# A hybrid encoder layer with 16,384 retrieved experts: other beats for the second sequence's stages

## The chip, the cores and the metric

One core of a Trainium2 chip runs the whole program. The metric is the time of one execution on the device, in microseconds (us). It is given as the median of the runs, and beside it stands the one execution that was profiled.

## What is computed

Two sequences of 512 tokens (width 1024) pass the same layer, in float32. The reference, cut to what matters here:

```python
def encoder_layer(x, ...):
    xn = rmsnorm(x, norm1_g)
    a, hy, gates = split(xn @ w_in)                       # 512, 1536, 2048 columns
    ya = multiscale_pool(a) @ w_pool_out
    yb = hyena_mixer(hy) @ w_hyena_out                    # short conv, FFT conv, products
    h = x + (sigmoid(gate_a) * ya + sigmoid(gate_b) * yb) @ w_o
    return h + peer(rmsnorm(h, norm2_g))

def peer_block(xb):                                       # 128 tokens
    s = einsum(q(xb), keys)                               # 8 heads, 2 x 128 scores each
    sv, si = top_k(s, 16); best, pos = top_k(all 256 pair sums, 16)
    idx, gate = ids of the 128 chosen experts, softmax(best)
    act = gelu(einsum('ted,td->te', u_tab[idx], xb)) * gate
    return einsum('te,ted->td', act, v_tab[idx])
```

## The kernel before

`first_sequence` runs the first sequence alone up to its keys' scores (0 to 629.7 us in the trace). `second_and_experts` then does two things at once: the layer of the second sequence, and the experts of all 1024 tokens, in 8 tiles of 128 tokens. It holds all that the change touches.

**Gathered tiles** (0, 1, 5, 6, 7). For each of 128 choices POOL fetches one row of `peer_u` per token (`fetch_u`, L1359, 512 KB) and DVE multiplies it with the tokens and sums (`dot`, L1686). The row of `peer_v` (`fetch_v`, L1369, 512 KB) is weighted and summed by PE: `quad` (L1472) takes four choices in 8 matmuls. There are 6 buffers for rows of u and 7 for rows of v.

**Dense tiles** (2, 3, 4). All 16,384 experts are computed, in 128 steps: `product` (L1435, 8 matmuls, a 512 KB block of the first table), a gelu on ACT, the weighting on DVE, and for four steps 6 `job`s (L1451, 4 matmuls each, blocks of `peer_v`), which DVE adds up (L1724). The weights of the 16,384 experts for these tiles are built before that, in 48 chunks of 8 tokens: DVE and ACT write one-hot rows (L1671, L1538, L1546), PE multiplies them (`gates`, L1423), ACT evicts.

**Beats.** Every engine's queue is written out by hand in a loop over beats `n`. Beat `n` fetches row `n` of u (640 in all) and row `n - LAG` of v (LAG = 134). So beats 0 to 133 fetch only u, beats 134 to 639 fetch both, and beats 640 to 773 only v. The queues are in order; a beat has no duration of its own.

**Ticks.** The stages of the second sequence stand in each queue by ticks of 1.5 us of nominal cost (`Walk.upto`): z (8 weight blocks), f (the transform), i (its inverse), a/x/mix (pools), ga/gb/o (24 weight blocks), r (16 half blocks), t2 (transposes), and at last q and s, after which DVE routes two heads for tiles 4 and 5 (`route_here`). `tick_of` says how many ticks stand before a beat, `beat_of` is its inverse:

```python
def tick_of(n, lag, rows):
    return min(n, lag) + 2 * max(0, min(n, rows) - lag) + max(0, n - rows)
```

The other work is placed in beats: `ROUTED` (tile, first beat, pace: one `route_head` each, L139 to L161), `RANKED_AT` (`chosen`: the pass that turns ranks into expert numbers, L167 to L190), `GATED_AT` (the softmax's sum), `CHUNK_AT` (the 48 chunks). `FIRST` is the tick of the first dense step, `PACE` the ticks between two, and the last falls 16 ticks ahead of `TICKS`.

## Time and profile before

| what | value |
|---|---|
| median of 3 runs | 3322.87 us |
| range of the runs | 3322.39 to 3337.04 us |
| profiled execution | 3342.03 us, its span 3340.2 us |
| mean granted TensorE clock | 0.939 |
| busy: PE, DVE, POOL, ACT | 2901.8, 1731.4, 1532.3, 554.3 us |
| DMA traffic | 1004.79 MB, mean 301 GB/s |

Busy times overlap: each engine has the whole span. The clock is the share of full speed that was granted. GB/s counts all queues together; the DMA share beside it is the mean busy share of the 16 DMA engines, and it can pass 1 when packets overlap.

### The profile page before, as it was taken

How to read it: one execution, taken by the hardware profiler on the slowest of the kernel's cores; microseconds unless marked ns; L12 is line 12 of the kernel's file. 1: busy time of each engine (PE TensorE's matmuls, PEld its weight loads, DVE VectorE, ACT ScalarE, POOL GpSimd, SP SyncE). 2: the span in 40 equal slices, each digit the busy share in tenths (PEclk: the TensorE clock that was granted, in tenths of full speed). 3: DMA queues.
4: the chain of work that ended last, by engine and by line, in shares of the span. 5: the costliest groups of instructions: out<-in, count | busy, mean ns of one | idle time of the engine just before them, and what ended most of it. 6: DMA issues, size and time to landing. Idle time of an engine off the chain costs nothing.

```text
span 3340.2 us, 29711 instructions
## 1 busy us (share of the span) xinstructions
PE 2901.8 (87%) x10143; PEld 1457.6 (44%) x10143; DVE 1731.4 (52%) x3842; ACT 554.3 (17%) x1188; POOL 1532.3 (46%) x1335
## 2 busy tenths in 40 slices
PE   5999989566779989855599999999999999999995
PEld 3656648222334445424244444444444444443331
DVE  4331028789984746688347744466644444441101
ACT  3211123000124535436100000000000000000000
POOL 2211112365555544436455555555556555553343
PEclk9999989778889989977799999999999999999998
DMA  3332353797888998868999999999989999997786
GB/s 129 117 104 72 123 179 107 247 354 237 269 327 305 350 387 327 320 252 320 389 360 390 369 382 377 385 400 385 380 326 384 395 371 376 386 366 288 278 295 229
DMA packets 343933, 1004.79 MB, mean 301 GB/s; under 512 B 31751, under 2 KB 114567, under 8 KB 341224
## 3 DMA queue, kind: packets, MB, share of 16 engines
q0 software_dynamic: 184320, 671.17, 53.4%
q1 hardware_dynamic: 157736, 306.57, 25.8%
q10 hardware_dynamic: 1728, 25.17, 1.9%
q8 instruction: 81, 1.33, 0.2%
q14 instruction: 68, 0.56, 0.0%
HBM read 950.62 MB, written 52.17 MB: 300 GB/s over the span
## 4 chain that ended last, share of the span: by engine, by line
PE 55%; DMA 8%; DVE 8%; issue 4%; ACT 3%; POOL 2%; another core or an unknown queue 1%; SPq 1%; DVEq 0%; ACTq 0%; POOLq 0%
PE job_ps L1451 19%; PE wide_ps L1435 18%; PE v_ps L1472 8%; PE wide_ps L579 3%; DMA v_rows<-in_peer_v,row_t 3%; DMA tmp_gates<-arena 2%; PE job_ps L579 2%; PE gate_ps L1423 2%; DVE prod L1686 2%; DMA u_row<-in_peer_u,row_u 2%; ACT arena L1546 1%; POOL u_row L1359 1%; ACT arena L1538 1%; DMA arena<-in_w_o 1%; DVE prod L186 1%
## 5 line engine op out<-in xcount | busy, mean ns | idle before, releaser
L1369 POOL DMA_INDIRECT v_rows<-in_peer_v,row_t x640 | 673.2, 1052 | 799.6 <-PE v_ps L1472 624.8
L1359 POOL DMA_INDIRECT u_row<-in_peer_u,row_u x640 | 736.5, 1151 | 487.3 <-DVE dots L1686 278.2
L1686 DVE CUSTOM_DVE_ANT_0 prod<-u_row,x_tile 128x1024 f32<-128x1024 f32 x640 | 766.2, 1221 | 88.3 <-DMA u_row<-in_peer_u,row_u 76.4
L1435 PE MATMUL wide_ps<-arena 128*128 128x384 f32 x2048 | 691.6, 492 | 32.0 <-DMA arena<-in_peer_ut 32.0
L1451 PE MATMUL job_ps<-arena 128*128 128x512 f32 x1536 | 692.7, 599 | 1.5 <-DVE arena L1724 0.9
L1435 PEld LDWEIGHTS wide_ps<-arena 128*128 128x128 f32 x2048 | 386.9, 191 | 353.7 <-issue 84.0
L1451 PEld LDWEIGHTS job_ps<-arena 128*128 128x128 f32 x1536 | 288.5, 191 | 377.3 <-issue 349.6
L1472 PE MATMUL v_ps<-v_rows,diag 128*32 128x512 f32 x2560 | 365.5, 619 | 54.5 <-DMA v_rows<-in_peer_v,row_t 37.4
L1724 DVE TENSOR_TENSOR arena<-arena,job_ps 128x512 f32<-128x512 f32 x192 | 131.9, 687 | 512.2 <-PE job_ps L1451 413.6
L843 POOL TENSOR_TENSOR exact<-arena,exact 128x1024 fp32r<-128x1024 f32 x48 | 117.8, 2457 | 445.2 <-ACT exact L591 445.2
L1572 ACT ACTIVATE arena<-wide_ps 128x384 f32<-128x384 f32 x128 | 62.7, 490 | 1492.8 <-PE wide_ps L1435 1218.9
L1712 DVE TENSOR_TENSOR arena<-arena 128x384 f32<-128x384 f32 x128 | 71.4, 558 | 374.8 <-ACT arena L1572 337.7
L579 PE MATMUL wide_ps<-arena 128*128 128x512 f32 x528 | 243.7, 618 | 18.0 <-DVE arena L785 18.0
L1472 PEld LDWEIGHTS v_ps<-v_rows,diag 128*32 128x32 f32 x2560 | 75.6, 111 | 286.2 <-issue 194.5
L579 PEld LDWEIGHTS wide_ps<-arena 128*128 128x128 f32 x528 | 103.6, 200 | 147.9 <-issue 147.7
L579 PE MATMUL job_ps<-arena 128*128 128x512 f32 x368 | 165.7, 605 | 0.0
L99 PE MATMUL pre_ps<-exact 128*128 128x512 f32 x384 | 159.5, 415 | 2.0 <-DVE exact L738 2.0
L1423 PE MATMUL gate_ps<-arena 128*128 128x128 f32 x640 | 99.0, 304 | 64.0 <-ACT arena L1561 42.8
L100 PE MATMUL pre_ps<-exact 128*128 128x512 f32 x384 | 151.1, 393 | 0.0
L101 PE MATMUL pre_ps<-exact 128*128 128x512 f32 x384 | 150.9, 393 | 0.0
L1423 PEld LDWEIGHTS gate_ps<-arena 128*128 128x128 f32 x640 | 90.2, 212 | 101.3 <-issue 93.2
L1546 ACT ACTIVATE arena<-arena,gate_t,gate_n 128x128 f32<-128x128 f32 x320 | 127.4, 482 | 0.9
(242 smaller groups left out, 2263.9 us busy)
## 6 DMA issues: line engine op xcount, KB each, us to landing
arena<-in_peer_ut SPq DMA_DIRECT2D x128, 512.0 KB
arena<-in_peer_v SPq DMA_DIRECT2D x128, 512.0 KB
arena<-in_w_in SPq DMA_DIRECT2D x64, 512.0 KB, 3.6
tmp_gates<-arena ACTq DMA_DIRECT2D x12, 2048.0 KB
arena<-tmp_gates SPq DMA_DIRECT2D x32, 768.0 KB
arena<-in_w_o SPq DMA_DIRECT2D x32, 512.0 KB, 3.6
arena<-in_wq SPq DMA_DIRECT2D x32, 512.0 KB, 4.7
u_row<-in_peer_u,row_u POOLq DMA_INDIRECT x640
```

Of the source, the lines that this page charges most:

```text
L99: pe.matmul(out, w_lo, m_hi, start=first, stop=False)
L100: pe.matmul(out, w_hi, m_lo, start=False, stop=False)
L101: return pe.matmul(out, w_hi, m_hi, start=False, stop=last)
L579: return pe.matmul(out, self.w_raw[r][:, c], moving[0][:, k], start=first, stop=last)
L1359: pool.indirect_dma_start(u_row[n % NU][:], None, dram["peer_u"], bass.IndirectOffsetOnAxis(row_u[g % 2][:, e:e + 1], 0)).then_inc(u_in[n ...
L1369: pool.indirect_dma_start(v_row[n % NV], None, dram["peer_v"], bass.IndirectOffsetOnAxis(row_t[g % 3][:, t:t + 1], 0)).then_inc(v_in[n % N ...
L1423: last = pe.matmul(gate_bank(c, u)[:].rearrange("p (a t) -> p t a", t=4)[:, v], hot_b[c % 2][:, 4 * u + v], hot_a[c % 2][:, 4 * u + v], st ...
L1435: last = pe.matmul(wide[j % 2][:, 0:TD], uw[j % NW][:, k * P:(k + 1) * P], x_t[:, k], start=k == 0, stop=k == KD - 1)
L1451: last = pe.matmul(job_ps[q % 2][:], actd[g % 2][:, jj, d * P:(d + 1) * P], vw[j % NO][:, half * 512:(half + 1) * 512], start=jj == 0, sto ...
L1472: last = pe.matmul(v_ps[half][32 * q:32 * q + 32, :], diag[:, q, 32 * c:32 * c + 32], v_row[r % NV][:, half * 512:(half + 1) * 512], start ...
L1546: last = act.activation(hot_b[c % 2][:, v], hot_b[c % 2][:, v], ACT.Relu, bias=gate_t[d % 2][:, t0 + v:t0 + v + 1], scale=gate_n[d % 2][:, ...
L1686: dve.tensor_tensor_reduce(out=prod[n % 2][:], in0=u_row[n % NU][:], in1=xb[g % 2][:], scale=1.0, scalar=0.0, op0=ALU.mult, op1=ALU.add, a ...
```

## The change

It changes what a beat stands for, and moves the work that is placed in beats. In beats 0 to 133 two ticks stand where one stood; in beats 134 to 639 two as before; after them one as before.

```diff
 def beat_of(tick, lag, rows):
-    if tick < lag:
-        return int(tick)
-    if tick < lag + 2 * (rows - lag):
-        return int(lag + (tick - lag) / 2)
-    return int(rows + tick - lag - 2 * (rows - lag))
+    return int(tick / 2) if tick < 2 * rows else int(rows + tick - 2 * rows)
 def tick_of(n, lag, rows):
-    return min(n, lag) + 2 * max(0, min(n, rows) - lag) + max(0, n - rows)
+    return 2 * min(n, rows) + max(0, n - rows)
...
-    TICKS = 2 * ROWS
+    TICKS = 2 * ROWS + LAG
...
-    ROUTED = ((2, 72, 8), (3, 134, 7), (6, LAST + 60, 5), (7, 420, 8))
-    RANKED_AT = (-1, 64, 133, 187, LAST + 1, LAST + 4, LAST + 104, 484)
-    GATED_AT = (1, 72, 140, 194, LAST + 3, LAST + 10, LAST + 110, 492)
+    ROUTED = ((2, 36, 6), (3, 92, 6), (6, LAST + 90, 8), (7, 420, 8))
+    RANKED_AT = (-1, 30, 82, 140, LAST + 1, LAST + 4, LAST + 156, 484)
+    GATED_AT = (1, 36, 90, 148, LAST + 3, LAST + 10, LAST + 162, 492)
...
-    CHUNK_AT = [144 + 3 * c for c in range(EARLY // 2)]
-    CHUNK_AT += [198 + 3 * c for c in range(EARLY // 2)]
+    CHUNK_AT = [94 + 3 * c for c in range(EARLY // 2)]
+    CHUNK_AT += [152 + 3 * c for c in range(EARLY // 2)]
     CHUNK_AT += [max(CHUNK_AT[-1] + 3, GATED_AT[4]) + 3 + c + c // 2 for c in range(EARLY // 2)]
...
-    FIRST = LAG + 2 * (CHUNK_AT[-1] + 6 - LAG)
+    FIRST = tick_of(CHUNK_AT[-1] + 6, LAG, ROWS)
```

Worked out, these beats move (the two functions carry `LAST`, the beat of the last unit, and `TURNED`, the one ahead of q):

| beat of | before | after |
|---|---|---|
| first q (`TURNED`) | 203 | 136 |
| last unit of the layer (`LAST`) | 248 | 181 |
| chunks 0 to 15, 16 to 31, 32 to 47 | 144 to 189, 198 to 243, 254 to 276 | 94 to 139, 152 to 197, 203 to 225 |
| first dense step | 282 | 231 |
| `FIRST`, `PACE` in ticks | 430, 6.32 | 462, 7.09 |
| last product | 726 | 722 |

No instruction is added or taken away. Line numbers of the changed kernel are 4 lower from here on (L1686 is L1682 there, L1472 is L1468, L1435 is L1431, L1451 is L1447, L1423 is L1419).

First place: DVE, between two stages of the transform (`prods` and `kf` lie in `diag`). Before:

```order
L781 TENSOR_TENSOR v_rows<-diag 128x512
L1686 ISA prod,dots<-u_row,x_tile 128x1024
L1686 ISA dots 128x1
L1686 ISA prod,dots<-u_row,x_tile 128x1024
L1686 ISA dots 128x1
L1686 ISA prod,dots<-u_row,x_tile 128x1024
L1686 ISA dots 128x1
L1686 ISA prod,dots<-u_row,x_tile 128x1024
L1686 ISA dots 128x1
L1686 ISA prod,dots<-u_row,x_tile 128x1024
L1686 ISA dots 128x1
L775 TENSOR_TENSOR diag<-wide_ps,diag 128x512
```

and now:

```order
L781 TENSOR_TENSOR v_rows<-diag 128x512
L1682 ISA prod,dots<-u_row,x_tile 128x1024
L1682 ISA dots 128x1
L1682 ISA prod,dots<-u_row,x_tile 128x1024
L1682 ISA dots 128x1
L1682 ISA prod,dots<-u_row,x_tile 128x1024
L1682 ISA dots 128x1
L775 TENSOR_TENSOR diag<-wide_ps,diag 128x512
```

Five dots stood between them, now there are two.

Second place: PE, in the stages ga, gb and o, whose weight blocks are L579. Before:

```order
L1423 MATMUL gate_ps<-arena 128x128 x4
L1472 MATMUL v_ps<-v_rows,diag 32x512 x8
L1423 MATMUL gate_ps<-arena 128x128 x4
L579 MATMUL wide_ps<-arena 128x512 x8
L1423 MATMUL gate_ps<-arena 128x128 x4
L579 MATMUL wide_ps<-arena 128x512 x8
L1423 MATMUL gate_ps<-arena 128x128 x4
L1472 MATMUL v_ps<-v_rows,diag 32x512 x8
L1423 MATMUL gate_ps<-arena 128x128 x4
L579 MATMUL job_ps<-arena 128x512 x8
```

and now:

```order
L1419 MATMUL gate_ps<-arena 128x128 x8
L579 MATMUL job_ps<-arena 128x512 x8
L1419 MATMUL gate_ps<-arena 128x128 x8
L579 MATMUL wide_ps<-arena 128x512 x8
L1419 MATMUL gate_ps<-arena 128x128 x4
L579 MATMUL wide_ps<-arena 128x512 x8
L1419 MATMUL gate_ps<-arena 128x128 x8
L579 MATMUL job_ps<-arena 128x512 x8
```

The quads (v_ps) are gone from these stages; the chunks' matmuls (gate_ps) are still in them.

Third place: PE in the dense stretch, some way in. Before:

```order
L1451 MATMUL job_ps<-arena 128x512 x4
L1435 MATMUL wide_ps<-arena 128x384 x8
L1451 MATMUL job_ps<-arena 128x512 x8
L1472 MATMUL v_ps<-v_rows,diag 32x512 x8
L1435 MATMUL wide_ps<-arena 128x384 x8
L1451 MATMUL job_ps<-arena 128x512 x8
L1472 MATMUL v_ps<-v_rows,diag 32x512 x8
L1451 MATMUL job_ps<-arena 128x512 x4
L1435 MATMUL wide_ps<-arena 128x384 x8
L1472 MATMUL v_ps<-v_rows,diag 32x512 x8
L1435 MATMUL wide_ps<-arena 128x384 x8
L1451 MATMUL job_ps<-arena 128x512 x8
```

and now:

```order
L1431 MATMUL wide_ps<-arena 128x384 x8
L1468 MATMUL v_ps<-v_rows,diag 32x512 x8
L1431 MATMUL wide_ps<-arena 128x384 x8
L1468 MATMUL v_ps<-v_rows,diag 32x512 x8
L1447 MATMUL job_ps<-arena 128x512 x8
L1431 MATMUL wide_ps<-arena 128x384 x8
L1468 MATMUL v_ps<-v_rows,diag 32x512 x8
L1447 MATMUL job_ps<-arena 128x512 x8
L1431 MATMUL wide_ps<-arena 128x384 x8
L1447 MATMUL job_ps<-arena 128x512 x4
L1468 MATMUL v_ps<-v_rows,diag 32x512 x8
L1431 MATMUL wide_ps<-arena 128x384 x8
```

A quad stands after fewer products and jobs. Counted over the whole order, 37 quads stand ahead of the first product before and 24 now; from there to the quad of beat 639 PE has 114 products, 165 jobs and 89 quads before, and 116, 168 and 102 now; after it 14 products, 27 jobs and 34 quads, and now 12, 24 and 34.

## Rows read from the trace of the kernel before

**Rows 1.** Busy time of the engines by stage, whole second half
```profile
core 0: us, PE busy (x) PEld busy (x) DVE busy (x) ACT busy (x) POOL busy (x), PEclk, DMA share, GB/s
629.70:793.90 164.20, 116.83 (x270) 52.62 (x268) 144.25 (x253) 8.81 (x13) 102.67 (x78) 0.85 0.88 317
793.90:906.00 112.10, 82.85 (x169) 35.31 (x170) 103.86 (x270) 10.12 (x14) 57.26 (x45) 0.84 0.81 269
906.00:1145.80 239.80, 209.28 (x750) 98.00 (x749) 164.26 (x397) 98.04 (x255) 133.44 (x114) 0.95 0.87 318
1145.80:1255.50 109.70, 89.37 (x325) 45.03 (x324) 62.76 (x98) 46.06 (x113) 51.43 (x47) 0.89 0.99 386
1255.50:1463.00 207.50, 184.69 (x810) 101.11 (x808) 139.16 (x450) 111.10 (x287) 97.52 (x86) 0.95 0.87 318
1463.00:1640.80 177.80, 68.65 (x389) 45.27 (x389) 123.54 (x252) 67.67 (x171) 86.07 (x74) 0.69 0.83 314
1640.80:3023.20 1382.40, 1357.06 (x4569) 632.93 (x4570) 706.31 (x1455) 67.30 (x127) 759.55 (x707) 0.99 0.99 376
3023.20:3340.20 317.00, 268.25 (x989) 101.23 (x987) 43.80 (x74) 12.41 (x24) 121.72 (x129) 0.95 0.75 270
```

**Rows 2.** Timeline of PE: start, us, engine, line, what; idle before it in brackets
```profile
701.53 1.97 PE L508 MATMUL wide_ps<-s_ident,arena 128*128 128x128 f32 x8 [18.24 <-DVE arena L754]
...
745.77 3.75 PE L527 MATMUL wide_ps<-arena,v_rows 128*128 128x512 f32 x4 [10.42 <-DVE diag L778]
...
793.88 6.65 PE L579 MATMUL wide_ps<-arena 128*128 128x512 f32 x10 [18.02 <-DVE arena L785]
```

**Rows 3.** Timeline of PE in the dense stretch: products, jobs, quads
```profile
1690.23 1.92 PE L1472 MATMUL v_ps<-v_rows,diag 128*32 128x512 f32 x16
1692.09 5.43 PE L1435 MATMUL wide_ps<-arena 128*128 128x384 f32 x16
1697.35 7.03 PE L1451 MATMUL job_ps<-arena 128*128 128x512 f32 x16
1704.22 5.32 PE L1435 MATMUL wide_ps<-arena 128*128 128x384 f32 x16
1709.38 3.60 PE L1451 MATMUL job_ps<-arena 128*128 128x512 f32 x8
```

**Rows 4.** Timeline of PE where the layer's last weights and the gates alternate
```profile
1103.92 7.03 PE L579 MATMUL job_ps<-arena 128*128 128x512 f32 x16
1110.79 1.05 PE L1423 MATMUL gate_ps<-arena 128*128 128x128 f32 x8
1111.78 0.64 PE L1472 MATMUL v_ps<-v_rows,diag 128*32 128x512 f32 x4
```

**Rows 5.** Timeline of DVE after the layer's last unit
```profile
1460.42 1.23 DVE L1686 CUSTOM_DVE_ANT_0 prod<-u_row,x_tile 128x1024 f32<-128x1024 f32 x1 [0.25 <-DVE rk_best_at L161]
...
1461.58 1.22 DVE L1686 CUSTOM_DVE_ANT_0 prod<-u_row,x_tile 128x1024 f32<-128x1024 f32 x1
...
1469.46 0.49 DVE L139 MAX8 rk_top<-arena 128x8 f32<-128x128 f32 x2
...
1475.23 0.29 DVE L167 CAST top_key<-rk_top_at 128x256 f32<-128x256 uint32 x1 [0.21 <-DVE rk_best_at L161]
...
1490.92 1.23 DVE L1686 CUSTOM_DVE_ANT_0 prod<-u_row,x_tile 128x1024 f32<-128x1024 f32 x1 [0.25 <-DVE key L190]
```

**Rows 6.** Timeline of POOL, one gather of a row per token
```profile
1609.24 0.94 POOL L1369 DMA_INDIRECT v_rows<-in_peer_v,row_t  x1 [0.30 <-issue]
```

**Rows 7.** Busy time in three full pieces of the dense stretch
```profile
2100.00:2150.00 50.00, 50.00 (x169) 23.82 (x169) 19.50 (x33) 2.45 (x5) 27.80 (x27) 1.00 1.03 403
2200.00:2400.00 200.00, 199.14 (x683) 92.20 (x681) 116.83 (x297) 7.84 (x16) 107.57 (x104) 1.00 1.01 388
2580.00:2600.00 20.00, 20.00 (x63) 9.07 (x62) 8.89 (x15) 0.98 (x2) 9.53 (x10) 1.00 1.03 410
```

**Rows 8.** Waits of PE after the last dot
```profile
PE v_ps L1472 <- DMA v_rows<-in_peer_v,row_t: 23.6, 24, 4.0
```

**Rows 9.** DMA queue of the gathers: packets, MB, share of 16 engines
```profile
q0 software_dynamic: 184320, 671.17, 53.4%
```

More of the change, by code:

```diff
@@ L1145, in second_and_experts @@
     EARLY = CHUNKS // ND * 2
-    ROUTED = ((2, 72, 8), (3, 134, 7), (6, LAST + 60, 5), (7, 420, 8))
-    RANKED_AT = (-1, 64, 133, 187, LAST + 1, LAST + 4, LAST + 104, 484)
-    GATED_AT = (1, 72, 140, 194, LAST + 3, LAST + 10, LAST + 110, 492)
-    assert 194 < LAST and LAST + 106 < 3 * P
-    CHUNK_AT = [144 + 3 * c for c in range(EARLY // 2)]
-    CHUNK_AT += [198 + 3 * c for c in range(EARLY // 2)]
+    ROUTED = ((2, 36, 6), (3, 92, 6), (6, LAST + 90, 8), (7, 420, 8))
+    RANKED_AT = (-1, 30, 82, 140, LAST + 1, LAST + 4, LAST + 156, 484)
+    GATED_AT = (1, 36, 90, 148, LAST + 3, LAST + 10, LAST + 162, 492)
+    assert 148 < LAST and LAST + 158 < 3 * P
+    CHUNK_AT = [94 + 3 * c for c in range(EARLY // 2)]
+    CHUNK_AT += [152 + 3 * c for c in range(EARLY // 2)]
     CHUNK_AT += [max(CHUNK_AT[-1] + 3, GATED_AT[4]) + 3 + c + c // 2 for c in range(EARLY // 2)]
```

## The prediction

> **What bounds the kernel now.** I read the busy time by stage first. It falls into two kinds. From 1640.8 to 3023.2 us, the dense stretch, PE is busy 1357 of 1382 us at a clock of 0.99 [rows 1]: PE is the bound. But the same row has a DMA share of 0.99 and 376 GB/s, so a second bound lies just behind. Ahead of it, from 629.7 to 1640.8 us, nothing is full for long: PE is busy 752 of 1011 us, DVE 738 (the first six rows of the group, summed), and they wait for each other. Until 906 us DVE is the fuller one (248 of 276 us, PE 200), because a dot stands in its queue for every 1.5 us of nominal stage work. The timeline of PE shows what that costs: 18.2, 10.4 and 18.0 us of idle time at the ends of z, f and i, each ended by a late DVE operation [rows 2]. From 906 to 1255.5 us PE is the fuller one (299 of 350 us), and from 1463 to 1640.8 us both wait: PE is busy 69 of 178 us.
>
> **Prices.** A product takes 5.16 us, a job 3.44 (two in 6.87), a quad 1.86, all from start to start [rows 3]. A weight block of the layer takes 6.87 us and half a chunk of gates 0.99, so a chunk about 1.95 [rows 4]. On DVE a dot takes 1.15 us, a routed head 5.8, a chosen pass 15.7 [rows 5]. A gather holds POOL for 0.94 + 0.30 us [rows 6] and moves 671.17 MB / 1280 = 0.524 MB [rows 9]. A dense step loads 1.245 MB: twice 512 KB, and a quarter of the 768 KB of gates for four steps.
>
> **The stretch up to the first q** takes 626 us now, with 203 dots, 17 quads and three chosen passes beside it. After the change 67 dots fewer (77 us of DVE), no quad (17 x 1.86 = 32 us of PE), and two chosen passes (16 us less). I go by stage.
> - z, f, i: 164.2 us now. PE's own work is 8 blocks (55 us) and 32 matmuls each for f and i, at a quarter of a job (27.5 us each), with the transposes 114. DVE has 39 dots in place of 78 (45 us less of 144). The chosen pass falls at beat 30, as i starts on PE: with nine dots, a head and the gate sum it is 33 us beside PE's 28 to 30, so the 18.0 us wait becomes about 5. I keep 20 us of the 50 in waits: **134**.
> - a, x, mix: DVE has 104 us in 112, of which 43 dots (50 us) and five heads (28). Now 21 dots (24), three heads (17) and the same 26: 67 us against PE's 59. They alternate closely, at the 0.87 that I take between them: **78**.
> - ga, gb, o: 239.8 us now. PE then has 165 us of blocks and 8 chunks (16), 181 in all, DVE about 150. The row has PE at 0.87 today; with the quads' row waits gone I take 0.91: **198**.
> - r and t2: 109.7 us now at 386 GB/s. PE's own work is 55 for r and 4 for t2, with seven chunks 73. Without the v rows the loads of w_o meet less traffic, and tile 3's chosen pass (16 us of DVE) has moved on: **94**.
>
> Sum 504, so 122 us less than 626. The bounds are 428 (PE alone: 399 us of stages and 15 chunks) and 549 (only the 77 us of dots gained).
>
> **q and s** still share two ticks per beat, 45 beats with both gathers, as before. One chosen pass and its gate sum come in (beat 140, 16 us), one chunk goes: 207.5 + 12 = **220**.
>
> **From the layer's end to the first product** there were 34 beats and now there are 50, since the second 16 chunks still stand beyond the layer's end in part and tile 4's 16 come after them. The 16 extra beats carry six chunks. POOL needs 2 x 1.24 = 2.5 us for each, the DMA 1.05 MB, 2.6 us at 400 GB/s, ACT some 2.7; I take 2.9. 178 + 46 = **224**. Here 46 us of the 122 are given back.
>
> So the first product starts at 629.7 + 504 + 220 + 224 = 1578, where it was 1641: **63 us earlier**.
>
> **The dense stretch** then has 51 beats more. PE: 116 x 5.16 + 168 x 3.44 + 102 x 1.86 = 1366 us, against 114, 165, 89: 1321, of the 1382 measured (0.956). At that share PE would need 1429, 47 us more. The DMA: today 376 x 1382 = 520 MB. Now 102 more gathers (53.5 MB) and two steps (2.5): 576 MB. What can the queues carry? The fullest 20 us show 410 GB/s, the fullest 50 us 403, the fullest 200 us 388, each at a share of 1.01 to 1.03 with PE at 100% [rows 7]. At 410 the 576 MB take 1405 us, which is above PE's 1366. **So the DMA takes over as the bound of this stretch.** At 403 it is 1429, at 388 1485. Between the dips at the tiles' borders and a queue that must not run dry, I take 395: 1458, rounded **1460**, 78 us more than now. Who waits then: dot waits for u rows, quad for v rows, and behind the waiting quad stand the products and jobs of PE.
>
> The Trainium skill (HBM Reference, Specifications) gives about 358 GB/s as a core's share, and about 425 for a core that streams alone. At 358 the stretch would take 1609 us and the change would be a clear loss; this trace has 376 over the whole stretch, so the lower figure does not bind here. At 425 it would be 1355 us, below PE's 1366, and PE would stay the bound; no 20 us of this trace show more than 410.
>
> **After the last dot** 12 products, 24 jobs and 34 quads are left where 14, 27 and 34 were: 2 x 5.16 + 3 x 3.44 = 21 us less of PE, in a stretch of 317 us where PE is busy 268 and waits 23.6 us in 24 pieces for v rows [rows 8]. A little of it turns into such waits: **20 us less**.
>
> **The sum**: -63 + 78 - 20 = -5 against the profiled execution, 3340.2 of span and 3342.0 in all. That one lies 19 us above the median (3322.9), 5 us above the highest of the runs; I take the same -5 from the median: **3318 us**.
>
> **Rivals.**
> 1. *The queues carry more than 403 GB/s* when they are asked for it, and PE stays the bound: 1429 instead of 1460, 31 us less, so 3287. For it: the shares never pass 1.03, and in the rows of 410 GB/s it was PE that was full, so nobody has asked for more. Against: three different pieces stop at 403 to 410. The same side is reached when the first stretch comes nearer to its PE bound: 480 instead of 504 gives 3294. Faster, together 0.36.
> 2. *The DMA gives 385*, as in the stages r and t2, where PE was busy only 89 of 110 us at a share of 0.99 [rows 1]: 576 / 385 = 1496, 36 us more than I take, so 3354. The mechanism is a queue of 6 and 7 buffers that stalls PE in order: a quad waits for four rows, and the products behind it wait too, so the loads of the next steps are issued later. It decides for slower from 390 GB/s down, given the other terms. Slower, 0.19.
> 3. *The DVE bursts stop PE in the first stretch*: two ticks per beat leave a unit of 6.87 us only 2.4 beats, and a head or a chosen pass in them is more than that slack. If PE's share there stays what it is today (498 of 626 us, 0.80), its 428 us take 535, 31 more than I have: 3349. Slower, 0.06.
> 4. My forecast, that the gain ahead of the first product is paid back behind it, 3301 to 3339: 0.39.
>
> **The chances.** A measurement of this kernel tells some 0.5% (16.6 us) from no change. Faster 0.36, same 0.39, slower 0.25. The range takes in 480 to 530 for the first stretch and 385 to 405 GB/s, not all at once: 3268 to 3360.
>
> **What the new profile would show.** Right: the first q at 1134 us, the last s at 1354, the first product near 1578, with DVE and PE both about 0.8 busy until the first q and no idle piece of 18 us before i's end is read. In the dense stretch PE below 0.95 busy, DMA 390 to 400 GB/s at 1.02, and DVE and PE waits for u and v rows many times the present ones; the last dot at 3038. Wrong: a dense stretch with PE at 0.98 (rival 1), or with less than 388 GB/s over it (rival 2), or a first q later than 1165 (rival 3). If the first product is not 40 to 85 us earlier, the first half of this working is what failed.

## The result, and the profile after

| | before | after |
|---|---|---|
| median (runs, range), us | 3322.63 (4, 3318.55 to 3337.04) | 3372.53 (4, 3362.45 to 3376.74) |
| ratio of the medians | | 1.0138, 95% interval 1.01 to 1.0176 |
| profiled execution, us | 3342.03 | 3362.45 |

The change makes the kernel 50 us slower. The forecast was 3318 and the range ended at 3360. The two profiled executions are 20 us apart and not 50: the one of before was 19 us above its median, the one of after 10 us below. So each kernel was profiled a second time; the stages of all four executions are below.

The stages of the changed kernel, cut at the same events as in [rows 1] (columns as there):

```profile
629.00:764.00 135.00, 112.68 (x269) 50.27 (x269) 98.54 (x176) 8.59 (x13) 51.71 (x42) 0.96 0.70 240
764.00:866.00 102.00, 97.13 (x212) 41.84 (x212) 85.38 (x222) 11.32 (x16) 38.71 (x30) 0.94 0.71 232
866.00:1015.40 149.40, 145.51 (x417) 70.67 (x416) 123.01 (x292) 56.05 (x143) 65.99 (x49) 1.00 0.76 262
1015.40:1118.40 103.00, 76.98 (x276) 43.33 (x274) 67.93 (x172) 61.31 (x156) 35.83 (x28) 0.90 0.85 318
1118.40:1319.50 201.10, 178.09 (x751) 93.03 (x752) 152.69 (x466) 96.57 (x244) 102.21 (x88) 0.94 0.87 325
1319.50:1554.40 234.90, 104.76 (x579) 62.17 (x577) 145.68 (x283) 104.92 (x276) 124.01 (x104) 0.70 0.85 320
1554.40:3058.80 1504.40, 1436.45 (x4853) 651.40 (x4853) 776.84 (x1570) 71.47 (x133) 893.86 (x810) 0.99 1.00 382
3058.80:3360.70 301.90, 249.55 (x914) 89.43 (x913) 40.15 (x70) 11.44 (x22) 121.26 (x129) 0.95 0.79 283
```

The seventh row is the one that counts. The dense stretch has grown from 1382 us to 1504, at 382 GB/s and a share of 1.00; PE is busy 0.955 of it, where it was 0.982. Ahead of it the change gains: the first product comes 86 us earlier. Laid beside the working (all in us; the pools and ga/gb/o stand together, because the border between them is not drawn at quite the same instruction in the two traces):

| stage | before | forecast | after | second execution: before, after |
|---|---|---|---|---|
| z, f, i | 164 | 134 | 135 | |
| a, x, mix, ga, gb, o | 352 | 276 | 251 | |
| r, t2 | 110 | 94 | 103 | |
| all ahead of the first q | 626 | 504 | 489 | 613, 493 |
| q, s | 208 | 220 | 201 | 208, 204 |
| to the first product | 178 | 224 | 235 | 177, 233 |
| dense stretch | 1382 | 1460 | 1504 | 1382, 1502 |
| after the last dot | 317 | 297 | 302 | 318, 304 |

In the second pair the sum is -67 ahead of the first product, +120 in the dense stretch and -14 after it: +39, and the times are 3327.58 and 3367.52.

In PE's timeline the three waits of [rows 2] read now (columns as there):

```profile
685.25 1.09 PE L508 MATMUL wide_ps<-s_ident,arena 128*128 128x128 f32 x8 [3.17 <-DVE arena L754]
...
723.44 1.95 PE L527 MATMUL wide_ps<-arena,v_rows 128*128 128x512 f32 x4 [3.10 <-DVE diag L778]
...
763.54 7.01 PE L579 MATMUL wide_ps<-arena 128*128 128x512 f32 x9 [12.29 <-DVE arena L785]
```

46.7 us have become 18.6. The first half of the change shortens these waits as intended.

The dense stretch is where the waits have grown. The waits there, first of the kernel before, then of the changed one (engine, tile, line, what it waited for: us in total, times, longest; PEld is PE's weight load):

```profile
PEld v_ps L1472 <- DMA v_rows<-in_peer_v,row_t: 16.6, 9, 4.8
DVE prod L1686 <- DMA u_row<-in_peer_u,row_u: 15.4, 9, 3.0
...
PE turn_ps L1391 <- DVEq L1646: 12.8, 2, 8.8
PE v_ps L1472 <- DMA v_rows<-in_peer_v,row_t: 10.7, 4, 3.9
```

```profile
POOL v_rows L1365 <- PE v_ps L1468: 342.8, 77, 31.7
...
DVE prod L1682 <- DMA u_row<-in_peer_u,row_u: 104.9, 65, 4.8
...
PEld v_ps L1468 <- DMA v_rows<-in_peer_v,row_t: 75.6, 38, 5.0
...
PE v_ps L1468 <- DMA v_rows<-in_peer_v,row_t: 44.3, 28, 4.1
PE turn_ps L1387 <- DVEq L1642: 16.1, 1, 16.1
```

A row of u is late 65 times where it was late 9 times, and a quad finds its rows missing 28 times in place of 4. POOL stands 343 us in front of gathers of v, because a quad on PE has not yet freed a buffer; in the kernel before that was 315 us. The row of PE's weight load says something that the row of PE hides. A quad needs four rows of v one after the other, and when the third or fourth is late, the wait can lie inside the quad and count as busy. In the grouping by line, the quads' matmuls take (busy, mean ns, idle before), in before and in after:

```profile
L1472 PE MATMUL v_ps<-v_rows,diag 128*32 128x512 f32 x1424 | 183.7, 605 | 10.9 <-DMA v_rows<-in_peer_v,row_t 10.7 <-issue 0.2
```

```profile
L1468 PE MATMUL v_ps<-v_rows,diag 128*32 128x512 f32 x1648 | 240.5, 608 | 44.3 <-DMA v_rows<-in_peer_v,row_t 44.3
```

1648 matmuls are 103 quads, and at 1.86 us each [rows 3] they need 192 us, not 240.5. That is 49 us more (before: 89 x 1.86 = 166 of 183.7, 18 us more). Some of it is waiting: the weight load waits 31 us longer for rows than the row of PE shows (75.6 and 44.3), and before only 6 us longer (16.6 and 10.7). The other 12 to 18 us are in both kernels.

Where in the stretch was traffic missing? Cut into five pieces:

```profile
1554.40:1854.40 300.00, 287.52 (x973) 130.78 (x974) 166.29 (x381) 14.86 (x28) 177.63 (x162) 0.98 1.02 392
1854.40:2054.40 200.00, 183.96 (x613) 82.34 (x612) 105.57 (x206) 10.24 (x18) 119.55 (x107) 0.98 0.95 362
2054.40:2454.40 400.00, 389.89 (x1324) 176.76 (x1323) 224.64 (x512) 18.31 (x35) 242.28 (x221) 1.00 1.02 394
2454.40:2604.40 150.00, 131.66 (x444) 60.82 (x443) 76.62 (x125) 8.10 (x14) 82.67 (x73) 0.94 0.88 334
2604.40:3058.80 454.40, 443.42 (x1506) 200.69 (x1504) 203.71 (x347) 19.96 (x38) 271.73 (x247) 1.00 1.01 389
```

Outside two holes the queues bring 392 GB/s (452 MB in 1154 us), close to the 395 of the working. In the holes, around the chosen passes of tiles 6 and 7, they bring 362 and 334: against 392 that is 200 x 30 + 150 x 58 = 14.7 MB, and 14.7 MB at 392 GB/s are 37 us. The two holes are as large as most of the 44 us by which this term was missed. The second lies around tile 7's pass, which the change does not touch (beat 484 in both kernels). The timelines of PE and of POOL there:

```profile
2477.99 1.92 PE L1468 MATMUL v_ps<-v_rows,diag 128*32 128x512 f32 x16
2496.03 0.47 PE L1387 MATMUL turn_ps<-s_ident,row_f 128*128 128x128 f32 x1 [16.12 <-DVEq L1642]
```

```profile
2481.44 1.62 POOL L1365 DMA_INDIRECT v_rows<-in_peer_v,row_t  x1 [0.30 <-issue]
2498.13 1.68 POOL L1355 DMA_INDIRECT u_row<-in_peer_u,row_u  x1 [15.07 <-DVE dots L1682]
```

While DVE turns ranks into expert numbers (15.7 us), it does no dot, no buffer of u comes free, and POOL stands 15 us in front of its next gather, with the gathers of v queued behind it. PE meanwhile waits 16 us for the row numbers that this pass makes. PE's idle piece as a window:

```profile
2480.00:2498.00 18.00, 1.97 (x4) 1.28 (x5) 17.45 (x23) 1.59 (x2) 2.56 (x2) 0.58 0.56 223
```

223 GB/s over 18 us. Whether such a hole is made up afterwards, the last experiments try. The pass isn't all that is in the holes: over the 200 and 150 us POOL also stands 34 and 26 us in front of gathers of v whose buffers the quads still hold, beside 16 and 21 us that DVE's dots keep it waiting.

After the last dot PE waits for rows of v as before: 25.6 us in 30 pieces, where it was 23.6 in 24 [rows 8].

```profile
PE v_ps L1468 <- DMA v_rows<-in_peer_v,row_t: 25.6, 30, 4.8
```

### The profile page after: what moved, and what is told of

Same layout as the page of the kernel before. It is cut to its first block, busy times and chain, and to the rows that moved or that the text cites. A ratio compares the mean times of both kernels' runs of the same rounds, so it can differ in the third digit from the quotient of the medians.

```text
span 3360.7 us, 29711 instructions
## 1 busy us (share of the span) xinstructions
PE 2927.5 (87%) x10143; PEld 1449.7 (43%) x10143; DVE 1733.3 (52%) x3842; ACT 554.6 (17%) x1187; POOL 1556.8 (46%) x1335
## 4 chain that ended last, share of the span: by engine, by line
PE 55%; DMA 12%; DVE 6%; POOL 3%; issue 2%; ACT 2%; SPq 0%; DVEq 0%; POOLq 0%; ACTq 0%
PE job_ps L1447 17%; PE wide_ps L1431 15%; DMA v_rows<-in_peer_v,row_t 10%; PE v_ps L1468 8%; PE wide_ps L579 6%; PE job_ps L579 4%; POOL v_rows L1365 2%; PE gate_ps L1419 2%; DMA tmp_gates<-arena 2%; POOL u_row L1355 2%; DVE prod L181 1%; DVE prod L186 1%; DVE prod L1682 1%; DVE key L190 1%; ACT arena L1542 1%
## 5 line engine op out<-in xcount | busy, mean ns | idle before, releaser
L1365 POOL DMA_INDIRECT v_rows<-in_peer_v,row_t x640 | 696.9, 1089 | 722.5 <-PE v_ps L1468 551.6
L1682 DVE CUSTOM_DVE_ANT_0 prod<-u_row,x_tile 128x1024 f32<-128x1024 f32 x640 | 766.6, 1220 | 159.7 <-DMA u_row<-in_peer_u,row_u 151.7
L1431 PE MATMUL wide_ps<-arena 128*128 128x384 f32 x2048 | 691.3, 491 | 33.6 <-DMA arena<-in_peer_ut 33.6
L1447 PE MATMUL job_ps<-arena 128*128 128x512 f32 x1536 | 691.3, 599 | 7.5 <-DVE arena L1720 7.5
L1431 PEld LDWEIGHTS wide_ps<-arena 128*128 128x128 f32 x2048 | 385.9, 191 | 357.4 <-issue 86.5
L1468 PE MATMUL v_ps<-v_rows,diag 128*32 128x512 f32 x2560 | 411.1, 631 | 88.4 <-DMA v_rows<-in_peer_v,row_t 88.3
L1447 PEld LDWEIGHTS job_ps<-arena 128*128 128x128 f32 x1536 | 287.3, 191 | 387.9 <-issue 359.5
L579 PE MATMUL wide_ps<-arena 128*128 128x512 f32 x528 | 241.6, 615 | 15.8 <-DVE arena L785 12.3
L1468 PEld LDWEIGHTS v_ps<-v_rows,diag 128*32 128x32 f32 x2560 | 79.7, 112 | 363.3 <-issue 198.7
L1419 PE MATMUL gate_ps<-arena 128*128 128x128 f32 x640 | 102.4, 310 | 99.3 <-ACT arena L1557 92.8
L579 PEld LDWEIGHTS wide_ps<-arena 128*128 128x128 f32 x528 | 103.1, 198 | 143.3 <-issue 139.5
L579 PE MATMUL job_ps<-arena 128*128 128x512 f32 x368 | 161.3, 592 | 0.0
L1419 PEld LDWEIGHTS gate_ps<-arena 128*128 128x128 f32 x640 | 91.7, 217 | 138.4 <-issue 125.3
## 6 DMA issues: line engine op xcount, KB each, us to landing
tmp_gates<-arena ACTq DMA_DIRECT2D x12, 2048.0 KB, 10.7
```

The source lines that it names most:

```text
L579: return pe.matmul(out, self.w_raw[r][:, c], moving[0][:, k], start=first, stop=last)
L1365: pool.indirect_dma_start(v_row[n % NV], None, dram["peer_v"], bass.IndirectOffsetOnAxis(row_t[g % 3][:, t:t + 1], 0)).then_inc(v_in[n % N ...
L1419: last = pe.matmul(gate_bank(c, u)[:].rearrange("p (a t) -> p t a", t=4)[:, v], hot_b[c % 2][:, 4 * u + v], hot_a[c % 2][:, 4 * u + v], st ...
L1431: last = pe.matmul(wide[j % 2][:, 0:TD], uw[j % NW][:, k * P:(k + 1) * P], x_t[:, k], start=k == 0, stop=k == KD - 1)
L1447: last = pe.matmul(job_ps[q % 2][:], actd[g % 2][:, jj, d * P:(d + 1) * P], vw[j % NO][:, half * 512:(half + 1) * 512], start=jj == 0, sto ...
L1468: last = pe.matmul(v_ps[half][32 * q:32 * q + 32, :], diag[:, q, 32 * c:32 * c + 32], v_row[r % NV][:, half * 512:(half + 1) * 512], start ...
```

## The experiments

Stage lengths below are of each run's profiled execution, in the order: ahead of the first q, q and s, to the first product, dense stretch. "Before" beside a ratio is the kernel before in runs on the same chip. Two executions of one kernel agree within 2 us in the dense stretch (1382 and 1382; 1504 and 1502), but within 13 us only in the kernel before ahead of its first q (626 and 613).

### What the traffic of the tables costs

The blocks of the two dense tables are loaded once for each buffer, and then used over and over. Of b_noload and a_noload the one was made from before, the other from after, so both compute the dense tiles from the first blocks over and over.

```diff
-    LOADS = sorted([(b, 0, j) for j, b in enumerate(LOAD_U_AT)] + [(b, 2, j) for j, b in enumerate(LOAD_V_AT)]
+    LOADS = sorted([(b, 0, j) for j, b in enumerate(LOAD_U_AT[:NW])] + [(b, 2, j) for j, b in enumerate(LOAD_V_AT[:NO])]
...
-                pe.wait_ge(uw_in[j % NW], 16 * (j // NW + 1))
+                pe.wait_ge(uw_in[j % NW], 16)
...
-                        pe.wait_ge(vw_in[j % NO], 16 * (j // NO + 1))
+                        pe.wait_ge(vw_in[j % NO], 16)
```

> The kernel before, with the blocks of the two dense tables loaded only for the first buffers (3 blocks of u, 6 of v) and used again for all 128 steps, so the dense tiles are computed from wrong blocks and some 125 MB of loads are gone; every matmul, dot, gather and DVE operation stays. Theory A (in the changed kernel's dense stretch the DMA is the bound, before it was PE): the dense stretch of the kernel before hardly moves, 1382 to 1365 to 1380 us, total -5 to -20 us. Theory B (the dense stretch is bound by PE and by the in-order waits between PE, DVE and POOL alone, not by traffic): the same, no move. This run is the base for the next one.

> The changed kernel with the same edit (dense table blocks loaded only for the first 3 and 6 buffers, the dense tiles computed from wrong blocks). Theory A: the stretch from the first product to the last dot, 1504 us in the changed kernel, falls to PE's need, 1366 us of work at 0.956 to 0.98 = 1395 to 1430, so 75 to 110 us, and the changed kernel without loads becomes faster than the kernel before without loads by 30 to 70 us. Theory B: the stretch stays within 20 us of 1504, and the changed kernel stays 20 to 50 us slower than the kernel before.

Measured: b_noload 3300.71 us beside 3323.12, ratio 0.9919 (0.9892 to 0.9946), stages 619, 200, 179, 1366. a_noload 3282.36, ratio 0.9866 (0.984 to 0.9892), stages 493, 200, 236, 1441. The dense stretch of both as windows, b_noload first:

```profile
1628.00:2993.00 1365.00, 1348.16 (x4565) 630.06 (x4566) 704.63 (x1453) 67.41 (x127) 761.79 (x707) 0.99 0.82 296
```

```profile
1560.00:3001.00 1441.00, 1408.03 (x4845) 648.50 (x4847) 772.07 (x1569) 71.38 (x133) 897.60 (x810) 0.99 0.88 318
```

Some 117 MB less are worth 16 us of the dense stretch to the kernel before and 61 to the changed one; by the ratios of the whole times, 0.8% and 2.7%. **Without them the order is turned round**: the changed kernel is then 18 us the faster, 3282.36 beside 3300.71. I had expected 30 to 70 us, and a dense stretch of 1395 to 1430; it took 1441. The edit takes away loads of tables and not the gathers that the change moves. So it shows that the traffic turns a gain into a loss, and not that the traffic is all that the longer dense stretch costs. Without the loads the change still lengthens it by 75 us (1366 to 1441), of which 45 are PE's own added work (1321 to 1366 in the working); with them by 120 to 122. The waits for rows go with the traffic: DVE's waits for rows of u fall from 104.9 us to 27.6 in a_noload, PE's for rows of v from 44.3 to 9.3.

Next only the first table's loads are left out of the changed kernel (of the first pair of lines above only the `[:NW]`, and the second pair). The products are again computed from the first blocks.

> The changed kernel with only the blocks of the first dense table loaded once (3 blocks, used for all 128 products, so the dense tiles are computed from wrong ones); the second table is loaded as ever. About 62 MB less, half of what the run without both loads left out. There the dense stretch was 1441 us, with both loads 1504. Hard bound (the time is the longer of PE's own and bytes over some 390 GB/s): 513 MB need 1315 us, so PE's own time shows in full and the stretch is 1441 to 1450, the total 3285 to 3297. Soft bound (the traffic slows every wait in proportion): half of the gain, 1470 to 1478 and a total of 3320 to 3335.

Measured: 3313.9 us beside 3327.59, ratio 0.9965 (0.9955 to 0.9975), stages 491, 201, 234, 1458.

```profile
1557.00:3015.00 1458.00, 1416.45 (x4853) 648.65 (x4851) 774.69 (x1569) 71.35 (x133) 894.42 (x810) 0.99 0.94 353
```

The three points (1441 us at 318 GB/s, 1458 at 353, 1502 at 383) show how the bound sets in. Length times rate gives 458, 515 and 575 MB. Going down from 575, the first 60 give 44 us, 0.73 us for each MB, and the next 57 give 17, 0.3 for each. By the ratios of the whole times (1.0138, 0.9965, 0.9866) the two steps are some 57 and 33 us, so the bend is less sharp there, and each step takes away another table's loads. Both steps pay, and no edge shows at which the DMA takes over from PE. The larger of PE's need (1429) and of bytes over the full pieces' 403 GB/s (1427 at most) would have been 1429 for all three. The measured 1458 lies between my two expectations, 1441 to 1450 for a hard bound and 1470 to 1478 for a soft one.

### The two kernels once more

> The kernel before once more, unchanged. If the 17 us between its first profiled execution and the median sit in one place, a stage is shorter by that much; if they are spread, no stage differs by over 8 us. Dense stretch 1370 to 1382 us.

> The changed kernel once more, for a second profiled execution: its first lay 10 us below its median, that of the kernel before 19 us above. If the loss sits in the dense stretch in every execution, that stretch is 1504 to 1515 us again and the first q comes within 5 us of 1118.

One execution each: 3327.58 and 3367.52 us; the stages are in the table above. The 13 us by which the profiled execution of before lay above its second one are all ahead of the first q, where DVE and PE wait for each other.

### Where the dense stretch starts

The first dense step comes 20 beats later:

```diff
-    FIRST = tick_of(CHUNK_AT[-1] + 6, LAG, ROWS)
+    FIRST = tick_of(CHUNK_AT[-1] + 26, LAG, ROWS)
```

> The changed kernel with the first dense step 20 beats later (FIRST from CHUNK_AT[-1] + 26 in place of + 6), all else the same; by the order 115 products stand between the first product and the last dot in place of 116, and 5 of the 102 quads move ahead of it. Theory A: from the layer's end to the last dot the bytes are the bound and stay the same, so the last dot comes within 10 us of where it is now and the total moves by 0 to +20 us. Theory B: PE has nothing but quads in the 20 beats, some 20 x 2.6 = 52 us at 9 us of work, and must do the same steps later: total +30 to +50 us.

Measured: 3364.85 us beside 3323.12, ratio 1.0119 (1.0088 to 1.0151), stages 489, 201, 274, 1459. The first product comes 39 us later and the last dot no later (2423 us after the first dot of the second half, against 2429 and 2432). An end that doesn't move when PE's dense work starts 20 beats later, with 5 of the 102 quads done ahead of it, is not set by PE alone.

### Where tile 6 is routed

Tile 6's heads, its pass and its gate sum go back to the beats that they had before:

```diff
-    ROUTED = ((2, 36, 6), (3, 92, 6), (6, LAST + 90, 8), (7, 420, 8))
+    ROUTED = ((2, 36, 6), (3, 92, 6), (6, 308, 5), (7, 420, 8))
```

> The changed kernel with tile 6's eight heads, its chosen pass and gate sum at the beats of the kernel before (308 every 5, 352, 358, in place of 271 every 8, 337, 343). Theory A (the map of the beats makes the loss): no move, within 8 us of 3370. Theory C (where the passes were put makes a good part of it, by a dip of 361 GB/s at 1854 to 2054 us): 15 us or more faster.

Measured: 3370.22 us beside 3327.59, ratio 1.0137 (1.0121 to 1.0153), dense stretch 1507. So where tile 6 is routed, the second cause that the diff offers for the longer dense stretch, isn't one.

### Fewer beats moved

One and a half ticks for each of the first 134 beats, so that 51 gathers of v move into the dense stretch and not 102, with routing and chunks placed between the two kernels' beats:

```diff
-    return min(n, lag) + 2 * max(0, min(n, rows) - lag) + max(0, n - rows)
+    return 1.5 * min(n, lag) + 2 * max(0, min(n, rows) - lag) + max(0, n - rows)
...
```

`beat_of` is changed to match. In r15, tile 4's last pair of heads is routed after its chosen pass, so that the pass reads what isn't there yet; r15f has `LAST` one beat later, which sets that right.

> Half of the change: 1.5 ticks per beat in the first 134 beats (1 before, 2 in the change), with routing, chosen and gate passes and chunks placed between the two versions; first dense step about beat 257, 30 quads ahead of the first product (37 before, 24 changed). If what is won ahead of the first product is paid back behind it at the same rate, the time lies half way: 3345 us +- 10. If there is an optimum between DVE-bound beats (before) and DMA-bound beats (changed), it is faster than both: 3290 to 3315: the first stretch loses its DVE waits as in the change (-50 us at the first product) while the dense stretch asks for only some 400 GB/s (+30 us).

> The map with 1.5 ticks per beat again, with everything that hangs on the layer's last beat one beat later, so that tile 4's last head is routed before its chosen pass (in the first version the pass came ahead of it). Time as there: 3318 to 3330, the same as the kernel before.

Measured: r15 3323.68 us beside 3323.12, ratio 0.9995 (0.9982 to 1.0007), stages 546, 212, 191, 1417. r15f 3323.35 beside 3327.59, ratio 0.9993 (0.998 to 1.0005), stages 550, 213, 199, 1430. Neither expectation for r15 came: it was neither half way (3345) nor faster than both (3290 to 3315). Half of the change takes 63 us off the first stretch (550 for 613), and by the medians all of it is paid back behind. The second half of the change gives another 57 us and costs 72 in the dense stretch (1430 to 1502). The profiled execution of r15f (3340.60) lies 17 us above its median and that of r15 (3315.03) 9 below, and their dense stretches differ by 13 us; so the 72 are good to some 13 us.

### The depth of the rows' buffers

One buffer more for rows of v and one less for rows of u, 13 in all as before, in after (a_nv8), before (b_nv8) and r15f (r15f_nv8):

```diff
-    NU, NV, NSC, NW, NO = 6, 7, 4, 3, 6
+    NU, NV, NSC, NW, NO = 5, 8, 4, 3, 6
```

> The changed kernel with one row buffer moved from u to v (5 and 8 in place of 6 and 7), all else the same; no byte more or less. Theory A1 (the queues carry no more bytes): the dense stretch stays 1504 +- 12 us and the total within 10 us of 3372; waits only move from PE to DVE. Theory A2 (with full queues a row lands later, and a quad, which needs four of seven buffers, hands that on to PE): PE's waits for v rows, 44 us in this stretch, fall to 25 or less, those of DVE for u rows rise from 105, and the total falls by 15 to 35 us.

> The same move of one buffer in the kernel before. There PE waits for v rows only 11 us in the dense stretch and 24 after it. Both theories: little, -10 to +10 us; a loss of up to 20 us in its first 134 beats is possible, where DVE waits for u rows and has one buffer less.

> The map with 1.5 ticks per beat and one row buffer moved from u to v (5 and 8). In the two kernels that move took 23 us off the stretch after the last dot, where PE waits for v rows; in the kernel before it cost some 10 to 20 us in the first 134 beats, where DVE is the bound, in the changed one nothing. With DVE less full there: 3300 to 3315, faster than both kernels.

Measured: a_nv8 3359.3 us beside 3333.85, ratio 1.008 (1.0052 to 1.0107), dense stretch 1507. b_nv8 3327.53, ratio 0.9981 (0.9965 to 0.9997), dense stretch 1387. r15f_nv8 3342.25 beside 3327.59, ratio 1.0054 (1.004 to 1.0069), stages 557, 210, 193, 1447. PE's waits for rows of v after the last dot in a_nv8, then POOL's waits for a buffer of u in its dense stretch:

```profile
PE v_ps L1468 <- DMA v_rows<-in_peer_v,row_t: 11.2, 20, 1.5
```

```profile
POOL u_row L1355 <- DVE dots L1682: 358.4, 102, 29.8
```

The buffer is worth some 20 us after the last dot (302 to 279 in after, 317 to 294 in before) and nothing in the dense stretch. There POOL's wait has only changed sides: 343 us for buffers of v have become 45, and 63 us for buffers of u have become 358. So one buffer moved from u to v doesn't help the dense stretch. Whether more buffers in all would, wasn't tried. The kernel before gives part of the gain back ahead of the first q (634). r15f_nv8 was a miss: I expected a gain, and by the medians it is 19 us slower than r15f. Its dense stretch is 17 us longer than that of r15f and 30 longer than that of r15, and DVE waits there 81.7 us for rows of u in place of 55.8 in r15f. That five buffers for u are too few there is the nearest reading, and it was not tried apart.

### The row numbers of tiles 6 and 7

PE turns a pass's result into row numbers four beats later, and DVE copies them four beats later too (`LATE` = 4; a_turn from after, b_turn from before):

```diff
-                    if e and tile in GATHERED and n == RANKED_AT[e] + 2:
+                    if e and tile in GATHERED and n == RANKED_AT[e] + 2 + (LATE if e >= 6 else 0):
...
```

> The changed kernel with PE's turn of the row numbers of tiles 6 and 7, and DVE's copy of it, 4 beats later (at the pass + 6 and + 9 beats, not + 2 and + 5), so that PE does not stand still for the DVE pass. Theory D (the dips are what is missing from the sum): PE's wait of 16.1 us goes and the total falls by 8 to 16 us. Theory E (the bytes bind, and PE only waits elsewhere): within 5 us of 3370.

> The same in the kernel before, where PE is the bound of the stretch and waits 12.8 us for the two passes: both theories -6 to -13 us, so 3310 to 3320 against some 3325.

Measured: a_turn 3367.56 us beside 3327.42, ratio 1.0112 (1.0084 to 1.014), dense stretch 1508. b_turn 3315.78, ratio 0.9961 (0.9948 to 0.9975), dense stretch 1370. In the changed kernel PE's wait of 16.1 us is gone and the dense stretch is no shorter; the ratio, 1.0112 beside 1.0138, moves less than the intervals are wide. POOL's timeline in a_turn shows what stayed:

```profile
2506.52 1.68 POOL L1356 DMA_INDIRECT u_row<-in_peer_u,row_u  x1 [15.07 <-DVE dots L1683]
```

It still stands for 15 us and asks for no rows. PE no longer waits in that time, but its waits for rows of v are no shorter: 47.3 us, where the two executions of the changed kernel have 44.3 and 33.5. In the kernel before, where PE is busy 0.98 of the stretch, the same edit takes 12 us off the dense stretch, which had 12.8 us of such waits. The same kind of wait removed is worth nearly all of its length in one kernel, and in the other nothing in the dense stretch.

### The pass in two halves

So the hole in the requests is filled: the pass of tiles 6 and 7 is cut in two halves, six beats apart, with dots between them, and the turning follows 12 beats after the start (`LATE` = 10). The cut of `chosen` itself is left out here.

```diff
...
-                        chosen(e)
+                        chosen(e, 0 if e >= 6 else None)
+                    if e >= 6 and n == RANKED_AT[e] + 6:
+                        dve.wait_ge(dot_done, n)
+                        chosen(e, 1)
```

> The changed kernel with the chosen passes of tiles 6 and 7 cut in two (heads 0 to 3, six beats later heads 4 to 7) and the turn 12 beats behind the start. A DVE burst is then 8.5 and 7.4 us in place of 15.7, about what six and seven row buffers can cover. Theory D: the dips in the DMA (361 and 313 GB/s) mostly fill, the dense stretch falls from 1504 to 1470 to 1485, total -15 to -35 us. Theory E: within 8 us of 3370.

> The same split in the kernel before. PE is the bound there: its wait of 12.8 us goes and some of the dearth of v rows after each pass: total -10 to -18 us, faster than both kernels. If it is not faster than b_turn, the burst itself costs nothing there and only PE's place in the order did.

Measured: a_split 3347.3 us beside 3327.42, ratio 1.006 (1.0041 to 1.0078), dense stretch 1482. b_split 3305.68, ratio 0.9931 (0.9908 to 0.9953), dense stretch 1365. In a_split, POOL's longest stand at the pass and the dense stretch as a window:

```profile
2482.36 1.68 POOL L1356 DMA_INDIRECT u_row<-in_peer_u,row_u  x1 [7.21 <-DVE dots L1692]
```

```profile
1559.00:3040.00 1481.00, 1431.70 (x4841) 652.01 (x4844) 774.76 (x1568) 71.39 (x133) 895.24 (x810) 0.99 1.01 388
```

15 us have become 7, and the stretch runs at 388 GB/s in place of 382, 20 to 22 us shorter: as much as half of the 44 that the forecast missed. The two holes as windows, in a_split:

```profile
1859.00:2059.00 200.00, 193.01 (x653) 86.58 (x652) 113.27 (x220) 10.23 (x18) 122.90 (x112) 1.00 1.00 383
2459.00:2609.00 150.00, 142.21 (x483) 63.38 (x482) 83.17 (x138) 11.35 (x18) 92.51 (x80) 0.98 0.95 362
```

383 for 362 and 362 for 334 GB/s are 4.2 MB each, together 8.4 MB, and at 392 GB/s 21 us: what the stretch gained. In both holes POOL's waits for buffers of v are as before (33 and 26 us); what has shrunk are its longest waits for dots, from 10.4 and 15.1 us to 4.8 and 7.2. a_turn had taken out the wait of PE alone without a gain in the dense stretch, so the likeliest source of what a_split gained are the gathers and not the turning, though a_split turns six beats later still.

In the kernel before, the split also does more than the turning: b_split is 10 us faster than b_turn by the medians (0.9931 beside 0.9961, intervals that overlap by their ends), 5 of them in the dense stretch. So the long pass seems to cost something there too, beyond PE's wait. The 22 us gained in all were more than the 10 to 18 expected.

The last two put the parts together.

> One and a half ticks a beat in the first stretch together with the chosen passes of tiles 6 and 7 cut in two halves. Bytes theory (the dense stretch is bound by what the queues bring, and a split pass evens out when rows are asked for): the first stretch keeps its gain of some 65 us, the dense stretch falls from 1430 to 1410, and the time is 3300 to 3308 us beside 3323 to 3328 of the kernel before, about that of the kernel before with split passes (0.9931). If the split acts through the first stretch's pace and not through the dense one, it adds nothing here: 3320 to 3326.

> The kernel before with split passes and with one buffer more for the second table's rows and one less for the first's. If the two gains lie in different stretches (dense and tail), they add: 0.9931 x 0.9981 = 0.9912 of the kernel before, about 3298 us. If the row buffers only moved work between stretches, 3303 to 3308, as with split passes alone.

Measured: r15f_split 3312.71 us beside 3324.14, ratio 0.9959 (0.9943 to 0.9974), stages 548, 211, 198, 1406. b_split_nv8 3296.91, ratio 0.9908 (0.9893 to 0.9923), stages 629, 201, 176, 1371. In r15f the split gives 24 us in the dense stretch of the profiled executions, but that of r15f was the one 17 us above its median; by the ratios (0.9993 and 0.9959) the split gives 11 us. The run is 5 us above the expected range and no better than b_split: the first stretch's gain is still paid back. b_split_nv8 is where the sum of the two gains had it, and it is the best version of this study, 27 us below the kernel before and 76 below the changed one. Its interval touches that of b_split, so the buffer's part isn't shown apart.

## Why the prediction was wrong

**The step that failed** is the dense stretch, "Between the dips at the tiles' borders and a queue that must not run dry, I take 395: 1458". It measured 382 GB/s and 1504 us, so that the term was +122 and not +78. The 576 MB were right (382 x 1504 = 575). The direction of this term was right too: the DMA, and no longer PE alone, sets the length of the stretch, with the waits where the text looked for them. The size was off in two ways. I took the rate from full pieces, and 395 is only 2% below the 403 of a 50 us piece and above the 388 of the 200 us in the same rows [rows 7] (other 200 us of that trace show up to 393), while the mean of the stretch was 376. Outside the holes 392 came; the two holes cost 37 us. And I had seen such a hole's cause: a chosen pass of 15.7 us [rows 5] stood in the working as DVE time, and its other price, that no gather of u is issued during it, didn't. The split passes show that price: 20 to 22 us of the changed kernel's dense stretch, and some 5 us of the other's beyond what the turning gives.

**Rival 2** described what happened, with 385 GB/s and 1496 us; it was given 0.19. Its mechanism was a queue of 6 and 7 buffers that stalls PE in order. The stalls in front of quads are there; blocks that come late to the next steps are not, since products and jobs wait for a block 0.3 us in the whole stretch. How much of the stalls is the buffers stays open: moving one from u to v left the stretch at 1507, and more in all weren't tried. What is shown is that rows were asked for late around DVE's passes; outside the two holes the share of the DMA is 1.01 to 1.02.

**Rival 1**, that the queues carry more than 403 when asked and PE stays the bound, did not come: the fullest 50 us of the changed kernel show 406 GB/s and those of its variants with all loads 405 to 407, no more than the two executions of the kernel before (405 and 407), and PE was busy 0.955 of the stretch. Its other way, a first stretch near 480, came in part (489 to 493). The Trainium skill (DMA: Bandwidth & Descriptors, Specifications) gives 435 GB/s as the ceiling of the fabric and 358 as a core's limit at the HBM. No 50 us of these kernels' dense stretches come nearer to the first than 407. The second doesn't bind here: the dense stretch has 382 as its mean over 1504 us.

**The first stretch** was forecast at 504 and took 489 to 493, and its reasoning held: z, f, i to 1 us, and no wait over 12.3 us. I was too careful with a, x, mix, ga, gb, o, 276 for 251: PE is busy 243 of these 251 us, 0.97, where I took 0.87 and 0.91. With fewer dots between them the stages hardly hold each other up. r and t2 took 9 us more than I had. I had reckoned on faster loads of w_o, and PE's waits for them are indeed gone (7.3 us before), but it waits 11.7 us for DVE in t2 and 9.9 us for ACT's part of the chunks. Rival 3, DVE bursts, didn't come.

**q and s, and the way to the first product**: 201 and 235, where 220 and 224 were forecast. The pass of 16 us that came in fitted beside PE's work: no wait of PE in q and s is put down to it, so I needn't have added it. The 16 extra beats cost 57 us, not 46; my 2.9 us for a beat had no row behind it. The two errors, -19 and +11, partly cancel, which is luck.

**After the last dot** -15 for -20, as the text had it.

**The anchor**: I took the difference of the profiled execution over to the median. Its first stretch was 13 us longer than in a second execution, and in the second pair the gain ahead of the first product is 67 us and not 86. That is 19 of the 30 us by which the medians' difference (50) exceeds the first pair's (20); the last 10 lie between the second pair (40) and the medians. Against the second pair the forecast's terms are -63 for -67, +78 for +120 and -20 for -14: 42 of the 44 us missed are the dense stretch.

So of the 55 us between forecast and result 44 are the dense stretch, 5 the tail; the rest of the profiled pair went the other way (-23), and the anchor brings back 30.

**Is the cause settled?** That traffic in the dense stretch makes the loss is shown by a_noload beside b_noload, where the change gains 18 us, and borne out by a_uonce and a_first20. That this traffic is above all the gathers moved in is reckoned from the bytes (53.5 of the 56 MB added); no run kept the change's order and left the moved gathers out. That cutting the long passes gives back some 22 of the missed 44 us is shown by a_split; that it acts through the gathers and not the turning is likely from a_split beside a_turn. What the other half is made of stays open: what is left of the holes, where POOL waits for buffers of v, and the 392 GB/s between them. Neither a version without any hole nor one with more buffers in all was tried.

## What to carry to other kernels

When a change moves traffic into a stretch that already runs at a DMA share of 0.99, work out the bytes at both rates, that of its full pieces and the mean of the whole stretch, dips included. Here they give 576 / 403 = 1429 and 576 / 376 = 1532 us, and 1504 came, nearer to the second; my 1460 was 44 too short. The mean was PE's pace as much as the DMA's, so it is a bound and not a forecast. A stretch with both PE and DMA near full has little slack to pay with. And where the DMA is near its bound, look for the long operations of the engine that frees the buffers: here cutting them up brought 20 us, and moving a buffer from one queue to the other nothing in that stretch.

## What the runs showed that I had not expected

- The bound bends over a wide range: the changed kernel's dense stretch gains 17 us between 353 and 318 GB/s, far below the 406 that its fullest 50 us reach. The kernel before, at 376, still had 16 us to gain.
- A removed wait of 16 us brought nothing in the dense stretch of one kernel, and 12.8 us of the same kind brought 12 in the other.
- The first stretch of the kernel before takes 612 to 626 us in kernels with the same order of instructions up to there (b_turn 612, b_again 613, b_split 618, b_noload 619, before 626), while that of the changed kernel is 489 to 493 in all nine profiled executions. So the stretch in which DVE and PE wait for each other has a spread of its own, and a profile shows one draw of it.
